# Gate projections from split operands and a new order of the middle part, in the two-layer stage of a one-core kernel

## The chip, the core and the metric

The kernel runs on one core of a Trainium2 chip. The metric is the device time of one execution in microseconds (us), given as the median of several runs. The engines are named as in the profile: PE (TensorE, matrix products), PEld (its weight loads), DVE (VectorE), ACT (ScalarE), POOL (GpSimd) and SP (SyncE, whose queue issues the DMAs here). An fp32 matmul leaves two records in the trace; a matmul of operands of type fp32r leaves one.

## What is computed

A model of two blocks on 256 tokens of width 1024. The first block (a mixer and a mixture of 32 experts) isn't touched by the change. The second block is two layers of this form:

```
def second_block(x, ...):
    for l in range(2):
        h = rms_norm_2(x, attn_norm_g[l])
        proj = h @ w_in[l]
        c_q, c_kv, k_rope, gq, gk, gv, pool_in, gate_logits = split_columns(proj, IN_SIZES)
        o_mla = mla_branch(c_q, c_kv, k_rope, ...)      # 8 heads of 96 (64 + 32 rotated)
        o_gqa = gqa_branch(gq, gk, gv, ...)             # 8 query heads of 64, 2 key heads
        o_pool = pool_branch(pool_in, w_pool[l], pool_scale[l])
        gates = jax.nn.sigmoid(gate_logits).reshape(b, s, 3, d)
        merged = (gates[:, :, 0] * (o_mla @ w_branch_mla[l])
                  + gates[:, :, 1] * (o_gqa @ w_branch_gqa[l])
                  + gates[:, :, 2] * (o_pool @ w_branch_pool[l]))
        x = x + merged @ w_out[l]
        hf = rms_norm_2(x, ffn_norm_g[l])
        u = depthwise_conv(hf @ ffn_w_up[l], ffn_conv_w[l], ffn_conv_b[l])
        x = x + (jax.nn.silu(u_gate) * u_val) @ ffn_w_down[l]
```

In both attention branches each query head and each key head is divided by its own root mean square, scaled by a gain and rotated; the softmax runs over all 256 tokens. All inputs and outputs are fp32.

## The kernel before

Activations lie with their channels over the partitions and the 256 tokens along the row, so a tile is 128 channels by 256 tokens. The layers start at 1237.7 us in the profiled execution and end with it. Five instruction streams are written out by hand, one for each engine, and meet by counting semaphores; no planner orders them.

**PSUM.** The list `order` (from L486) names every filling of one of the eight banks in the order in which PE makes them, and the engine (ACT or DVE) that takes it out. Banks go round; `lay(name)` on PE waits until the bank's last content is taken. `full(name)` on ACT and DVE waits for PE.

**Fills of a layer**, in PE's order: `ss1` and `cq`, `ckv` (latents), `gq0`, `gq1`, `gk`, `gv`, `po0`, `po1`; sums of squares `sslat`, `ssg0`, `ssg1`, `ssgk`; `ga0`, `ga1`; `uq0` to `uq3` (the mla queries), `uk0` to `uk3`, `uv0`, `uv1`; `swg0`, `swg1`, `swgk` (partners for the rotation of gq and gk); `pl0`, `pl1`; `ga2`; `ssq0` to `ssq3`; `ga3`, `ga4`; `ssk0` to `ssk3`; `ga5`, `ga6`; `swq0` to `swq3`, `swk0` to `swk3`; `ga7`; then the attention loop. A step i of that loop makes the scores of head i, the transposes of head i-2, in steps 0 to 3 also the gate `ga(8+i)`, and every second step the outputs of two heads. After it come the branch products `br`, the output projection `wo`, and the feed-forward part with `up0` to `up21` and `dn0` to `dn3`.

**Gates.** `gates(n)` makes one of twelve pairs of tiles of the gate logits: 2 x 8 fp32 matmuls of 128x128 weights by 256 tokens. They need only h and their weights. ACT takes them out with a tanh.

**Norms.** For queries and keys alike PE sums the squares of a head over the partitions with a matrix of ones, so that the sum stands in every partition; DVE takes mean and reciprocal over [96, 8 x 256] (mla) or [128, 6 x 256] (gq and gk), ACT takes the root, DVE multiplies the head by it. In the loop DVE takes the maximum of a head's scores (`tensor_reduce`), negates and scales it (`nmax`), ACT takes the exponential with an immediate scale and the negated maximum as bias, and sums it.

**Split operands.** The up and down projections are already made from split operands: ACT rounds a unit of weights to fp32r (`w_hi`, two buffers), DVE subtracts (`w_lo`), and PE adds hi*hi, hi*lo and lo*hi. ACT may write a buffer when PE has done with its last content.

**Weights in the ring.** `Stream` lays the pieces of weights one after another into a ring of LRING = 16384 columns and wraps; SP loads a piece when those under it are used (`used`), strictly in order. Pieces of a layer without such a predecessor in the same layer are loaded ahead (`early`): `w_lat`, `w_gq`, `w_gkv`, `w_pool`, `w_uq`. A `gate` piece holds three gates (3 MB), an `up` piece two fills (2 MB).

## Time and profile before

| | |
|---|---|
| median of 3 runs | 2229.58 us (2224.77 to 2230.18) |
| the profiled execution | 2224.29 us, its span 2222.5 us |
| mean granted clock of PE in it | 0.989 |
| PE busy | 2122.2 us, 95% |
| DVE busy | 812.7 us, 37% |
| ACT busy | 540.9 us, 24% |
| the layers | from 1237.7 us to the end |

The chain of work that ended last is PE for 69% of the span. A row of the order of time gives start, duration, engine, line, operation, what it writes and reads, shape, count, and in brackets the idle time before it with what ended it. The last records' ends of PE are modelled, so the spacing of starts tells more than the duration of one.

### The profile page before, as it was taken

The numbers are of one execution on the slowest core, as the hardware profiler recorded it, in microseconds if no ns is written. First come the engines' busy times: TensorE is split into PE (matmuls) and PEld (weight loads), VectorE is DVE, ScalarE is ACT, GpSimd is POOL, SyncE is SP. The second block draws the span as 40 slices with busy tenths as digits, with TensorE's granted clock in tenths as the row PEclk, the third lists the DMA queues.
The fourth block names the chain that finished last, engine by engine and source line by source line (L and its number), as shares of the span: only waits on it lengthen the run. The fifth ranks groups of instructions, "written<-read, shape, count | busy, mean of one in ns | idle before, by whom it ended". The sixth has DMA issues, their size and how long they took to land.

```text
span 2222.5 us, 29751 instructions
## 1 busy us (share of the span) xinstructions
PE 2122.2 (95%) x11486; PEld 1333.1 (60%) x11487; DVE 812.7 (37%) x1468; ACT 540.9 (24%) x905; POOL 25.3 (1%) x45
## 2 busy tenths in 40 slices
PE   6998999999999999999999999999999999999999
PEld 4763333333333333333333787778999887688999
DVE  3521221122222112221121348434885258425874
ACT  1421111111111111111111122312663132403653
POOL 0000000000000000000000020000000020000000
PEclk8998999999999999999999999999999999999999
DMA  9686997099999999999899334316551633325551
GB/s 347 254 353 255 410 419 303 1 381 418 418 417 417 417 419 418 418 418 418 334 417 411 106 114 152 114 40 199 178 194 53 199 112 118 114 97 169 190 176 53
DMA packets 210004, 580.05 MB, mean 261 GB/s; under 512 B 23264, under 2 KB 124896, under 8 KB 173952
## 3 DMA queue, kind: packets, MB, share of 16 engines
q1 hardware_dynamic: 209920, 578.83, 67.9%
q8 instruction: 65, 1.06, 0.2%
q14 instruction: 19, 0.16, 0.0%
HBM read 577.48 MB, written 1.31 MB: 260 GB/s over the span
## 4 chain that ended last, share of the span: by engine, by line
PE 69%; DMA 10%; SPq 8%; DVE 8%; ACT 3%; issue 2%; ACTq 0%; DVEq 0%
PE bank L756 16%; PE bank L1017 13%; DMA ring<-in_w_gu 9%; PE bank L1068 8%; SPq L630 4%; SPq L632 4%; PE bank L1340 3%; PE bank L1342 3%; PE bank L1341 3%; PE bank L980 3%; PE bank L994 3%; DVE heap L2104 2%; PE bank L826 2%; DMA ring<-in_w_in 2%; PE bank L1356 1%
## 5 line engine op out<-in xcount | busy, mean ns | idle before, releaser
L1017 PE MATMUL bank<-ring,heap 128*64 128x512 f32 x2304 | 519.2, 601 | 23.9 <-DMA ring<-in_w_gu 23.8
L1017 PEld LDWEIGHTS bank<-ring,heap 128*64 128x64 f32 x2304 | 158.0, 138 | 367.2 <-issue 289.2
L756 PE MATMUL bank<-heap,ring 128*128 128x256 f32 (+1 forms) x1600 | 350.5, 380 | 5.3 <-DVE heap L2148 3.2
L756 PEld LDWEIGHTS bank<-heap,ring 128*128 128x128 f32 (+1 forms) x1600 | 301.0, 189 | 51.5 <-DVE heap L2148 4.0
L1939 DVE TENSOR_SCALAR heap<-bank 128x256 f32<-128x256 f32 x36 | 15.3, 425 | 744.9 <-PE bank L1017 744.9
L1068 PE MATMUL bank<-ring,heap 128*64 128x512 f32 x1152 | 255.1, 595 | 0.0
L1340 PE MATMUL bank<-h_hi,w_hi 128*128 128x256 f32 x640 | 181.7, 284 | 3.4 <-DVE w_lo L2161 3.4
L1342 PE MATMUL bank<-h_hi,w_lo 128*128 128x256 f32 x640 | 181.1, 283 | 0.0
L1341 PE MATMUL bank<-h_lo,w_hi 128*128 128x256 f32 x640 | 181.1, 283 | 0.0
L2161 DVE TENSOR_TENSOR w_lo<-ring,w_hi 128x2048 fp32r<-128x2048 f32 (+1 forms) x64 | 142.4, 2226 | 97.7 <-ACT w_hi L1635 97.7
L1068 PEld LDWEIGHTS bank<-ring,heap 128*64 128x64 f32 x1152 | 79.3, 137 | 150.2 <-issue 144.2
L1491 ACT ACT_TABLE_LOAD x32 | 41.1, 1283 | 485.5 <-DVE heap L1939 485.0
L1635 ACT ACTIVATE w_hi<-ring 128x2048 fp32r<-128x2048 f32 (+1 forms) x64 | 119.1, 1861 | 145.2 <-PE bank L1342 85.5
L1340 PEld LDWEIGHTS bank<-h_hi,w_hi 128*128 128x128 f32 x640 | 122.8, 192 | 3.9 <-DVE w_lo L2161 3.8
L1341 PEld LDWEIGHTS bank<-h_lo,w_hi 128*128 128x128 f32 x640 | 122.8, 192 | 0.1
L1342 PEld LDWEIGHTS bank<-h_hi,w_lo 128*128 128x128 f32 x640 | 122.8, 192 | 0.0
L1356 PE MATMUL bank<-f_hi,w_hi 128*128 128x256 f32 x352 | 100.0, 284 | 1.0 <-DVE w_lo L2161 1.0
L1357 PE MATMUL bank<-f_lo,w_hi 128*128 128x256 f32 x352 | 99.6, 283 | 0.0
L1358 PE MATMUL bank<-f_hi,w_lo 128*128 128x256 f32 x352 | 99.6, 283 | 0.0
L1505 ACT ACTIVATE heap<-bank 128x512 f32<-128x512 f32 x36 | 21.5, 598 | 231.5 <-PE bank L1068 231.5
L980 PE MATMUL bank<-heap 128*64 128x512 f32 x296 | 73.4, 617 | 3.5 <-DVE heap L1899 3.5
L994 PEld LDWEIGHTS bank<-heap 64*128 64x128 f32 x592 | 54.1, 186 | 35.8 <-issue 29.2
(299 smaller groups left out, 2321.9 us busy)
## 6 DMA issues: line engine op xcount, KB each, us to landing
ring<-in_w_gu SPq DMA_DIRECT2D x256, 1024.0 KB, 18.8
ring<-in_w_down SPq DMA_DIRECT2D x128, 1024.0 KB, 19.8
ring<-in_ffn_w_up SPq DMA_DIRECT2D x44, 1024.0 KB, 7.7
ring<-in_w_ada SPq DMA_DIRECT2D x24, 1024.0 KB, 10.6
ring<-in_w_in SPq DMA_DIRECT2D x24, 1024.0 KB, 7.9
ring<-in_ffn_w_down SPq DMA_DIRECT2D x16, 1024.0 KB, 6.0
ring<-in_w_in SPq DMA_DIRECT2D x7, 2048.0 KB, 12.2
ring<-in_w_out SPq DMA_DIRECT2D x6, 2048.0 KB, 12.8
```

Source lines behind the costliest of these rows:

```text
L756: last = mm(outp, w(k), x(k), start=k == 0, stop=k == nk - 1)
L980: last = mm(psum[2][both[f], :], pick[:, t, FEW * r:FEW * (r + 1)], htok[:, t, 512 * f:512 * (f + 1)], start=t == 0, stop=t == TT - 1)
L994: last = mm(acc_of(f, c), y_sb[both[f], P * c:P * (c + 1)], sgT[both[f], :], start=False, stop=True, skip_group_check=True)
L1017: last = mm(psum[g][both[f], :], xgT[:, k % 4, k // 4, :], wt[:, g, :, f, :], start=False, stop=k == DT - 1, skip_group_check=True)
L1068: last = mm(psum[2][both[f], :], hidT[:, o:o + FEW], wt[:, 512 * f:512 * (f + 1)], start=k == 0, stop=k == DT - 1)
L1340: mm(b[:, g, :], wh, h_hi[:, k, :], start=k == 0, stop=False)
L1341: mm(b[:, g, :], wh, h_lo[:, k, :], start=False, stop=False)
L1342: last = mm(b[:, g, :], wl, h_hi[:, k, :], start=False, stop=k == DT - 1)
L1356: mm(b[:, a, :], wh, f_hi[:, k, :], start=k == 0 and a == 0, stop=False, skip_group_check=True)
L1357: mm(b[:, a, :], wh, f_lo[:, k, :], start=False, stop=False, skip_group_check=True)
L1635: f(hi, src, ACT.Copy).then_inc(S["whi"].sem, 1)
L2161: v.tensor_tensor(lo, src, hi.bitcast(F32), ALU.subtract).then_inc(S["wlo"].sem, 1)
```

## The change

1. **Gates from split operands.** `gates(n)` now makes three products of fp32r operands: 48 matmuls. Before it, ACT rounds the piece `ga{n}` to `w_hi` (`lead_gate`) and DVE makes `w_lo` (`rest_gate`). h itself is split once per layer. `lead_gate(n+2)` follows on ACT when gate n is taken out.
2. **Query norms.** Queries are multiplied by their gain only. Their sums of squares are made with tokens over the partitions (`by_query`: the squares as weights, one or two columns of ones), [128, 16] for all heads; reciprocal and root are taken of that, and the factor (with 1/sqrt of the head size) becomes the scale of the exponential and of `nmax`. Keys keep their norm.
3. **New order** of the fills between `uv1` and the attention loop, and of DVE's and ACT's work to match. DVE's steps between the `rest_gate` calls, which the diff below leaves out, are: before `rest_gate(1)` the mean and reciprocal of `sslat`; before `rest_gate(2)` cq and ckv scaled, mean and reciprocal of `ssgq` and `ssgk`, gq times its gain, gk scaled; before `rest_gate(4)` the means of `ssk0` to `ssk3`; before the long reciprocal the products of `swg0`, `swg1`, `swgk` and of `swq0` to `swq3` with the sine table; before `rest_gate(6)` mk scaled, the pool outputs, gq and gk times cosine and the sums; before `rest_gate(7)` the same for mq; after it `swk0` to `swk3` and the rotation of mk. Each `rest_gate` waits for its `lead_gate`.
4. **Smaller ring**: LRING = 10240; a gate, branch, output or half query/pool piece is 1 MB. `early` is now `w_lat`, `w_gq0`, `w_gq1`. The exponentials, their transposes and h lie in buffers of other steps. The down projection's four banks are 3, 4, 5, 6.

```diff
-LRING = 16384
+LRING = 10240
+NG = 12
@@ order of the fills
-                 ("gv", "act"), ("po0", "act"), ("po1", "act"), ("sslat", "dve"), ("ssg0", "dve"), ("ssg1", "dve"),
+                 ("gv", "act"), ("po0", "act"), ("po1", "act"), ("sslat", "dve"), ("ssgq", "dve"),
                  ("ssgk", "dve"), ("ga0", "act"), ("ga1", "act")]
         order += [(f"uq{i}", "act") for i in range(4)] + [(f"uk{i}", "act") for i in range(4)]
-        order += [("uv0", "act"), ("uv1", "act")] + [("swg0", "dve"), ("swg1", "dve"), ("swgk", "dve")]
-        order += [("pl0", "dve"), ("pl1", "dve"), ("ga2", "act")] + [(f"ssq{i}", "dve") for i in range(4)] + [("ga3", "act"), ("ga4", "act")]
-        order += [(f"ssk{i}", "dve") for i in range(4)] + [("ga5", "act"), ("ga6", "act")]
-        order += [(f"swq{i}", "dve") for i in range(4)] + [(f"swk{i}", "dve") for i in range(4)] + [("ga7", "act")]
+        order += [("uv0", "act"), ("uv1", "act"), ("ssq", "dve"), ("ga2", "act")] + [(f"ssk{i}", "dve") for i in range(4)]
+        order += [("swg0", "dve"), ("swg1", "dve"), ("swgk", "dve")] + [(f"swq{i}", "dve") for i in range(4)]
+        order += [("pl0", "dve"), ("pl1", "dve"), ("ga3", "act"), ("ga4", "act"), ("ga5", "act")]
+        order += [(f"swk{i}", "dve") for i in range(4)] + [("ga6", "act"), ("ga7", "act")]
...
+        def gate_unit(n):
+            hi, lo = (x[:, n % 2, :].rearrange("p (a b) -> p a b", a=DT) for x in (w_hi, w_lo))
+            return piece(lay_stream, f"ga{n}", DT), hi, lo
@@ used(name): when a piece may be overwritten
+            if name.startswith("ga"):
+                return S["wlo"], int(name[2:]) + 1
@@ PE
                 def gates(n):
-                    if n % 3 == 0:
-                        arrived(f"gate{n // 3}")
-                    w = piece(lay_stream, f"gate{n // 3}", 8, 3)
+                    done("wlo", n + 1)
+                    _, hi, lo = gate_unit(n)
                     b = halves(lay(f"ga{n}"))
                     for a in range(2):
-                        last = product(b[:, a, :], lambda k: w[:, k, n % 3, P * a:P * (a + 1)], h, DT)
+                        for k in range(DT):
+                            wh, wl = hi[:, k, P * a:P * (a + 1)], lo[:, k, P * a:P * (a + 1)]
+                            mm(b[:, a, :], wh, h_hi[:, k, :], start=k == 0, stop=False)
+                            mm(b[:, a, :], wh, h_lo[:, k, :], start=False, stop=False)
+                            last = mm(b[:, a, :], wl, h_hi[:, k, :], start=False, stop=k == DT - 1)
...
+                def by_query(name, slots, rows, sums):
+                    b = lay(name)
+                    n = 2 * NH // (TT * slots)
+                    for t in range(TT):
+                        for i in range(slots):
+                            o = NH * t + n * i
+                            last = mm(b[:, o:o + n], rows(i)[:, P * t:P * (t + 1)], sums, start=True, stop=True)
+                    last.then_inc(lay_full.sem, 1)
@@ ACT
+                def lead_gate(n):
+                    src, hi, _ = gate_unit(n)
+                    act.wait_ge(*lay_in.here(f"ga{n}", l))
+                    f(hi, src, ACT.Copy).then_inc(S["whi"].sem, 1)
                 def gates(n):
                     o = 8 * (n % 3) + 2 * (n // 3)
                     out_of(f"ga{n}", L["gates"][:, o:o + 2, :], func=ACT.Tanh, scale=0.5)
+                    if n + 2 < NG:
+                        lead_gate(n + 2)
...
                 for i in range(4):
-                    out_of(f"uq{i}", L["mq"][0:MQ, 2 * i:2 * i + 2, :], lambda b: two(b)[0:MQ])
+                    b = two(full(f"uq{i}"))[0:MQ]
+                    f(L["mq"][0:MQ, 2 * i:2 * i + 2, :], b, ACT.Identity, scale=v2("q_head", 0)[0:MQ])
+                    f(L["sq"][0:MQ, 2 * i:2 * i + 2, :], b, ACT.Square).then_inc(lay_drained["act"].sem, 1)
...
-                        f(pr[:, 0, :], b[:, 0, :], ACT.Exp, scale=scale, bias=st[:, 2:3], accum_out=st[:, 4:5])
+                        f(pr[:, 0, :], b[:, 0, :], ACT.Exp, scale=scale[:, 0:1], bias=st[:, 2:3], accum_out=st[:, 4:5])
@@ DVE, from the latent sums on
+                rest_gate(0)
...
+                rest_gate(1)
...
+                rest_gate(2)
+                taken(mean(rq[:, 0, :], full("ssq")[:, 0:2 * NH], MQ))
+                v.reciprocal(rq[:, 0, :], rq[:, 0, :]).then_inc(S["qvar"].sem, 1)
+                rest_gate(3)
...
+                rest_gate(4)
...
+                v.reciprocal(L["rs"][0:MQ], L["rs"][0:MQ]).then_inc(S["kvar"].sem, 1)
+                rest_gate(5)
...
+                rest_gate(6)
...
+                rest_gate(7)
...
                 for i in range(2 * NH + 1):
                     if i < 2 * NH:
                         b = full(f"s_{att[i]}")
                         c.step(v.tensor_reduce(st[:, 0:2], two(b), AX.X, ALU.max))
-                        v.tensor_scalar(st[:, 2:4], st[:, 0:2], -scale, None, ALU.mult).then_inc(S["nmax"].sem, 1)
+                        v.scalar_tensor_tensor(out=st[:, 2:4], in0=st[:, 0:2], scalar=-1.0, in1=scale, op0=ALU.mult,
+                                               op1=ALU.mult).then_inc(S["nmax"].sem, 1)
+                    if i < 4:
+                        rest_gate(8 + i)
                     if i >= 1:
                         out_act(f"s_{att[i - 1]}")
```

## Rows read from the trace of the kernel before

**Rows 1.** The page, part 1: busy us, share of the span, instructions
```profile
PE 2122.2 (95%) x11486; PEld 1333.1 (60%) x11487; DVE 812.7 (37%) x1468; ACT 540.9 (24%) x905; POOL 25.3 (1%) x45
```
**Rows 2.** Stretches: us, PE, PEld, DVE, ACT, POOL busy, PEclk, DMA, GB/s
```profile
1290.00:1424.05 134.05, 128.99 (x580) 105.21 (x578) 81.39 (x61) 35.51 (x52) 12.08 (x18) 0.99 0.31 103
1781.00:1915.00 134.00, 128.94 (x579) 105.26 (x577) 81.40 (x61) 35.50 (x52) 12.08 (x18) 0.99 0.31 103
```
**Rows 3.** Order of time, PE in both layers: start, us, what, [idle before]
```profile
1311.77 7.15 PE L756 MATMUL bank<-heap,ring 128*96 128x256 f32 x32 [0.55 <-DVE heap L2028]
...
1335.49 3.62 PE L756 MATMUL bank<-heap,consts_sb 96*96 96x256 f32 x16
1338.95 13.98 PE L756 MATMUL bank<-heap,ring 128*128 128x256 f32 x64
...
1356.61 5.38 PE L756 MATMUL bank<-heap,consts_sb 96*96 96x256 f32 x16 [3.69 <-ACT heap L1598]
...
1380.09 3.69 PE L558 MATMUL bank<-heap,consts_sb 96*96 96x256 f32 x16 [0.82 <-DVE heap L2028]
...
1847.66 5.38 PE L756 MATMUL bank<-heap,consts_sb 96*96 96x256 f32 x16 [3.69 <-ACT heap L1598]
```
**Rows 4.** A stretch after the wait of 3.69 us, as in rows 2
```profile
1358.00:1360.00 2.00, 2.00 (x6) 1.28 (x6) 1.20 (x2) 1.98 (x3) 0.00 (x0) 0.50 0.02 4
```
**Rows 5.** Order of time, PE at the first split products of the up projection
```profile
1546.40 0.28 PE L1341 MATMUL bank<-h_lo,w_hi 128*128 128x256 f32 x1
...
1557.68 0.28 PE L1342 MATMUL bank<-h_hi,w_lo 128*128 128x256 f32 x1
```
**Rows 6.** Order of time, ACT and DVE: splitting a unit of weights
```profile
1555.39 1.90 ACT L1635 ACTIVATE w_hi<-ring 128x2048 fp32r<-128x2048 f32 x1
...
1561.95 2.29 DVE L2161 TENSOR_TENSOR w_lo<-ring,w_hi 128x2048 fp32r<-128x2048 f32 x1
```
**Rows 7.** Order of time, PE: products with 32 columns, two records each
```profile
167.65 0.38 PE L964 MATMUL bank<-heap,consts_sb 128*128 128x32 f32 x2 [0.21 <-issue]
167.86 0.39 PE L965 MATMUL bank<-heap,consts_sb 128*128 128x32 f32 x2
```
**Rows 8.** Order of time, DVE: key norm's reciprocal; maximum and negation of scores
```profile
1362.75 12.95 DVE L2104 RECIPROCAL heap<-heap 96x2048 f32<-96x2048 f32 x1
...
1399.95 0.69 DVE L2127 TENSOR_REDUCE heap<-bank 128x2 f32<-128x512 f32 x1 [5.17 <-PE bank L1267]
1400.67 0.17 DVE L2128 TENSOR_SCALAR heap<-heap 128x2 f32<-128x2 f32 x1
1400.75 0.16 DVE L2132 RECIPROCAL heap<-heap 128x2 f32<-128x2 f32 x1
```
**Rows 9.** Lines 1660 and 1614 (durations ns min/median/max); ACT between two heads
```profile
L1660 ACT ACTIVATE heap<-bank,vec x80: 541/554/563, 1557.2 to 2157.0; 128x256 f32<-128x256 f32 x80
L1614 ACT ACTIVATE heap<-bank,heap x32: 476/476/477, 1394.9 to 1943.6; 128x256 f32<-128x256 f32 x32
1433.59 0.48 ACT L1614 ACTIVATE heap<-bank,heap 128x256 f32<-128x256 f32 x1 [1.29 <-DVE heap L2128]
```
**Rows 10.** PE's waits of 3.17 and 2.04 us, and stretches after waits (PEclk)
```profile
215.04 0.79 PE L1009 MATMUL bank<-bias_hi,bias_sel 64*128 64x512 f32 x1 [3.17 <-issue]
219.00:221.00 2.00, 2.00 (x8) 0.51 (x6) 0.00 (x0) 0.00 (x0) 0.00 (x0) 0.50 0.39 156
1231.56 1.10 PE L1109 MATMUL bank<-heap,consts_sb 128*128 128x256 f32 x4 [2.04 <-ACT heap L1526]
1231.50:1235.00 3.50, 2.36 (x9) 1.49 (x10) 3.50 (x13) 2.53 (x4) 0.00 (x0) 1.00 1.04 380
```
**Rows 11.** Line 695, four of the five w_gkv DMAs of each layer
```profile
DMA to landing us min/median/max: 4.4/9.2/13.7
```
**Rows 12.** The page, part 6: issues, KB each, median us to landing
```profile
ring<-in_ffn_w_up SPq DMA_DIRECT2D x44, 1024.0 KB, 7.7
ring<-in_w_in SPq DMA_DIRECT2D x24, 1024.0 KB, 7.9
```

## What I expect of the change, and why

> **What bounds the kernel now.** I read the busy shares of the page, then the stretches by stage, then the order of time on PE, DVE and ACT inside a layer. TensorE is busy 95% of the span [rows 1]. The change touches the layers alone, and there I look at the part from the squared sums to the last gate projection, 1293.4 to 1424.05: PE is busy for 129.0 of 134.1 us, DVE for 81.4, ACT for 35.5, and the second layer repeats it to a tenth [rows 2]. PE stands still three times in it, 0.55, 3.69 and 0.82 us, for DVE or ACT [rows 3]. After the 3.69 us its granted clock is 0.50, the 1.2 GHz level [rows 4], and 16 records take 5.38 us where 16 like them took 3.62 [rows 3]: 1.76 more. So PE sets the time, and DVE's chain of norms already touches the path.
>
> **The change part by part**, for one layer; the two layers double it.
>
> *Gates.* Two gate projections, 64 records, take 13.98 us [rows 3], 6.99 each. Three products of split operands are 48 records. The up projection has this form: from its second matmul at 1546.40 to its 96th at 1557.68 lie 94 starts [rows 5], 0.12 us each, so 5.76 per gate. Twelve gates: 12 x 1.23 = 14.8 us off PE. Each gate adds 1.90 us on ACT (the rounded half) and 2.29 on DVE (the rest) [rows 6], 22.8 and 27.5 together. The split of h adds as much once, while PE works on the pool projection and DVE has nothing else: no cost.
>
> *Query norms.* The gq sums go from 4 matmuls to 8 with two columns, the mq sums from 8 to 16 with one column. Nearest row: weights of 128x128 with 32 columns, two records in 0.21 us, 0.107 each [rows 7]. gq: 8 x 0.2185 = 1.75 becomes 16 x 0.107 = 1.71. mq: 5.38 becomes 32 x 0.107 = 3.42. Ends: 7.0 if a record cost as much as one of 256 columns (0.2185), 1.7 if it cost half of the nearest row; I take 3.42, the row with weights of the same width. Saved: 2.0. On DVE one of the two 12.95 us reciprocals [rows 8], its four means and its scaling go, and most of the one for gq/gk; tiny ones replace them. The factor now enters the exponential as a second operand per partition: activations out of PSUM with two such operands take 554 ns, with one 476 [rows 9]. That is 0.16 per head on ACT, which idles 1.29 ahead of a pair [rows 9]: no cost; without that cover 16 heads x 0.16 = 2.5. The Trainium skill (ScalarE: Activation LUTs, on what an ACTIVATE costs) gives about 93 ns for each such operand. By it the uncovered price would be 3.0; the rows have 78 ns.
>
> *Old waits.* 0.55 + 3.69 + 0.82 = 5.1 us go: the latent norm no longer stands behind the gq/gk reciprocal, the mk squares and the mk norm no longer behind those of mq.
>
> What goes: 14.8 + 2.0 + 5.1 = 21.9 us per layer, 43.8 in all.
>
> *New waits.* Every gate now waits for DVE's rest, so DVE's order counts. I lay the new order on layer 0's clock. PE: sums until 1297.3 as before, gates 0 and 1 until 1308.8 (their rests are ready at 1284 and 1301), uq 7.0, uk 3.6, uv 1.8, ssq 3.4, gate 2 5.8, ssk 3.5: 1333.9. From there DVE carries the chain: mean 0.7, rest of gate 4 2.2, three swg 1.9, four swq 2.4, reciprocal of mk 12.9 [rows 8], rest of gate 5 2.3: 1356.3. PE meanwhile does swg, swq and pool (7.8) and gates 3 and 4 (11.5), is ready for gate 5 at 1353.3 and waits 3.0. Then mk scaled 2.3, pool 1.6, rotation of gq/gk 3.6, rest of gate 6 2.3: 1366.0, PE waits 0.4. Rotation of mq 4.5, rest of gate 7 2.3: 1372.7, PE waits 1.0. swk and rotation of mk until 1379.6, when PE has just done the first scores. If the clock falls after the 3.0 wait, the lost 1.76 goes into the next two waits and leaves 0.4.
> The first four attention steps are the worst place. PE issues the scores of head i and then gate 8+i; on DVE the rest of gate 8+i stands behind maximum and negation of these same scores, and behind it stand the normalisation of the head before and that head's transposes. From the end of the scores: 0.72 + 0.08 + 2.29 = 3.1 us [rows 6, 8]. In steps 0 and 1 PE has nothing beside it; in steps 2 and 3 the transposes cover 0.5. New waits: 3.1 + 3.1 + 2.6 + 2.6 = 11.4, where the kernel before had none.
> All new waits are 3.0 + 0.4 + 1.0 + 11.4 = 15.8, with the 0.4 left over 16.2. Gained: 21.9 - 16.2 = 5.7 us per layer; the last gate would end at 1418.4.
>
> *The clock.* What does a wait of 3.1 or 2.6 us cost beyond itself? After waits of 3.17 and 3.69 the granted clock was 0.50, after one of 2.04 it was 1.00 [rows 4, 10]. 3.1 lies beside 3.17; 2.6 lies halfway. I take 2.5 half-speed stretches per layer in these four steps, at 1.76 each: 4.4 us. Bounds: none, or all four (7.0). Left: 5.7 - 4.4 = 1.3 per layer, 2.6 in all.
> The Trainium skill (TensorE: Matmul & The Clock Gate, on HAM oscillation) warns of idle gaps between short bursts of matmuls that put the engine back to half rate each time. It speaks against this change, and the 5.38 us row agrees.
>
> *Smaller ring.* 10240 columns hold five pieces of 1 MB. w_gkv is no longer loaded ahead: it waits for ckv and is needed two tile pairs (14.0 us) later. Its 256 KB DMAs landed 4.4 to 13.7 us after issue, beside other loads [rows 11]. With five issues of about 1 us ahead of the last, 5 + 9.2 would just miss, but those landings were in a crowded queue; alone I take 5 + 5: no cost. At worst 5 + 13.7 - 14.0 = 4.7 per layer. Behind it in SP's queue stand w_po0, w_po1 and gate 0, each needed 8 us or more after issue, against a median of 7.9 for such pieces [rows 12]. The third up piece now waits for up1, done at 1546.4; its user on ACT started at 1555.39 [rows 5, 6]; median landing 7.7 [rows 12]: no cost, at worst (13.7) 4.7. Later up pieces have some 17 us, three units of 5.76, between release and use.
>
> *The rest.* The new banks of the down projection, the exponentials and their transposes in the places of rs and sq, and branch and output weights in halves keep order and work: nothing. The three-operand negation on two elements: 0 to 0.1 us a head.
>
> **The sum.** The profiled execution took 2224.3 us (span 2222.5); 2224.3 - 2.6 = 2221.7 on that footing. The median of the three runs, 2229.6, lies 5.3 above it, so I forecast 2229.6 - 2.6 = 2227.0. A difference below 0.3% (6.7 us) can't be told from none here.
>
> **The rivals.**
> (a) The waits stay but the clock doesn't fall: 11.4 gained, 2218.2. For it: the 2.04 row. Against it: the 3.17 row. Chance 0.24.
> (b) PE never waits for the rests, and all 43.8 come: 2185.8. DVE's order as written speaks against it. Chance 0.04.
> (c) The other side: in the first four attention steps each wait is followed by a half-speed stretch like the one after 3.17 us, which held from 215 to 221 [rows 10], worth 3.0. Eight waits x 3.0 = 24.0 against 11.4: 12.6 slower, 2242.2. It decides from 18.1 (11.4 + 6.7), six such waits. The one-column sums, 3.4 us of weight loads with hardly a column, could add 1.76 per layer. Against it: the two 3.69 waits inside the layers lost 1.76 each. Chance 0.12.
> (d) The smaller ring starves PE at w_gkv and at the third up piece: 2 x (4.7 + 4.7) = 18.8 against 2.6: 16.2 slower, 2245.8. Chance 0.08.
>
> **How the numbers follow.** The forecast has 0.52: 2227.0, own range 2221 to 2236 (all four stretches in both layers, -11.4 + 14.1, and 3.5 for the one-column sums give +6.2). Faster: (a) and (b), 0.28. Same: the forecast, 0.52. Slower: (c) and (d), 0.20. The range takes in (a) with the runs' spread of 5 below it, and reaches toward (c): 2214 to 2238, which leaves out (b), (d) and most of (c).
>
> **What would show it.** Gate records start 0.12 apart; 384 f32 records per layer give way to 576 split ones. PE waits for the rests some 16 us per layer: 3.1, 3.1, 2.6 and 2.6 in the first four attention steps, about 3 before gate 5; after some of them slices at 0.50. uq starts near 1308.8, the last gate ends between 1418 and 1425. The prediction is wrong if PE doesn't wait in those four steps, if the clock stays at 1.00 after 3.1 us, or if PE waits for the ring.

## The result, and the profile after

The changed kernel takes 2232.25 us at the median of 20 runs (2224.51 to 2238.12), the kernel before 2229.34 (2223.9 to 2231.06, 20 runs). The ratio is 1.002, interval 1.001 to 1.0029: some 4.5 us slower (2.2 to 6.5). The forecast was 2.6 us faster. The time lies in the range given, but the direction was wrong. By the bound of 0.3% it is no difference; by the interval it is a small loss.

The profiled execution took 2233.18 us against 2224.29 for the one of before. Of these 8.9 us, 1.1 lie ahead of the layers (the first projection of layer 0 starts at 1238.78 instead of 1237.67), 3.8 in the first layer up to its branch products and 3.9 from there to the same point of the second layer. The rest lies behind that. The profiled execution of before was quick beside its 20 runs. So the layers are the place, and both show nearly the same loss.

The page of the kernel after, part 1, to be read beside [rows 1]:
```profile
PE 2110.7 (95%) x11918; PEld 1345.7 (60%) x11919; DVE 822.4 (37%) x1486; ACT 586.7 (26%) x939; POOL 31.1 (1%) x45
```
PE has 432 records more: 2 x 192 for the gates and 2 x 24 for the query sums. It is nevertheless busy for 11.5 us less. What was taken off it came back as waits and as time at half speed (time at half speed counts as busy).

PE's waits after, from the middle of the expert part to the end (waiting line, releaser, us in total, times, longest):
```profile
PE bank L1167 <- DVE w_lo L2101: 30.5, 12, 3.3
...
PE bank L1180 <- DMA ring<-in_w_in: 0.2, 1, 0.2
```
L1167 is the first product of a gate, L2101 DVE's rest: 30.5 us in twelve waits. Before, this wait did not exist. PE itself waits for a transfer only once in the layers, for 0.2 us; before it was 0.5. The ring of 10240 columns shows in one other place. In layer 0 ACT waits 0.38 us for the third up piece, and PE, which waits for that piece's rest at the first up product, waits 2.19 us where it waited 1.72 before:
```profile
1560.77 1.91 ACT L1669 ACTIVATE w_hi<-ring 128x2048 fp32r<-128x2048 f32 x1 [0.38 <-DMA ring<-in_ffn_w_up]
...
1565.06 0.39 PE L1362 MATMUL bank<-h_hi,w_hi 128*128 128x256 f32 x1 [2.19 <-DVE w_lo L2220]
```

Order of time on PE in layer 0 after (start, us, line, [idle before]):
```profile
1309.92 7.07 PE L770 MATMUL bank<-heap,ring 128*96 128x256 f32 x32
...
1322.34 4.51 PE L1218 MATMUL bank<-consts_sb,heap 96*128 96x1 f32 x32
...
1334.73 3.62 PE L770 MATMUL bank<-heap,consts_sb 96*96 96x256 f32 x16
...
1360.52 0.39 PE L1167 MATMUL bank<-h_hi,w_hi 128*128 128x256 f32 x1 [2.89 <-DVE w_lo L2101]
...
1376.86 0.39 PE L1167 MATMUL bank<-h_hi,w_hi 128*128 128x256 f32 x1 [0.70 <-DVE w_lo L2101]
...
1382.00 0.28 PE L1167 MATMUL bank<-h_hi,w_hi 128*128 128x256 f32 x1
1382.36 0.28 PE L1167 MATMUL bank<-h_hi,w_hi 128*128 128x256 f32 x1
...
1387.21 0.58 PE L1167 MATMUL bank<-h_hi,w_hi 128*128 128x256 f32 x1 [3.28 <-DVE w_lo L2101]
...
1388.02 0.41 PE L1167 MATMUL bank<-h_hi,w_hi 128*128 128x256 f32 x1
1388.66 0.41 PE L1167 MATMUL bank<-h_hi,w_hi 128*128 128x256 f32 x1
...
1400.06 0.58 PE L1167 MATMUL bank<-h_hi,w_hi 128*128 128x256 f32 x1 [3.18 <-DVE w_lo L2101]
...
1411.75 0.38 PE L1167 MATMUL bank<-h_hi,w_hi 128*128 128x256 f32 x1 [2.60 <-DVE w_lo L2101]
...
1422.01 0.38 PE L1167 MATMUL bank<-h_hi,w_hi 128*128 128x256 f32 x1 [2.60 <-DVE w_lo L2101]
...
1427.94 1.13 PE L1290 MATMUL bank<-heap 64*128 64x256 f32 x4
```
The upper rows are uq, the one-column sums and, behind gate 2, the first of the key sums. The waits stand where they were forecast, at gates 5 and 7 and at gates 8 to 11. L1167 is every third record of a gate: in gate 7 two such starts lie 0.36 us apart, 0.12 per record, and in gate 8, behind the wait of 3.28, they lie 0.64 apart.

Stretches of the same layer after (from:to, length, PE, PEld, DVE, ACT and POOL busy, granted clock, DMA share, GB/s):
```profile
1320.00:1334.00 14.00, 14.00 (x81) 12.66 (x80) 2.57 (x3) 6.92 (x9) 0.00 (x0) 0.76 0.49 151
1356.00:1366.00 10.00, 7.11 (x59) 6.91 (x58) 10.00 (x9) 5.60 (x4) 0.00 (x0) 1.00 0.44 130
1384.00:1396.00 12.00, 8.79 (x49) 8.66 (x50) 3.05 (x3) 2.54 (x6) 0.00 (x0) 0.72 0.28 87
1398.00:1410.00 12.00, 9.10 (x56) 8.34 (x56) 4.13 (x6) 3.80 (x8) 0.00 (x0) 0.86 0.29 89
1410.00:1428.00 18.00, 13.65 (x105) 12.76 (x105) 6.29 (x8) 3.82 (x11) 0.00 (x0) 1.00 0.34 118
```
A mean clock of 0.72 over 12 us means (1 - 0.72) x 12 / 0.5 = 6.7 us at 1.2 GHz. In this way: 6.7 us at the one-column sums and gate 2 (PE busy throughout!), none behind the 2.89 us at gate 5, 6.7 behind the 3.28 us at gate 8, 3.4 behind the 3.18 us at gate 9, none behind the two of 2.60. The second layer has the same three stretches. In the trace's record of the clock the lengths are 6.83, 6.83 and 3.41 us, so 17.1 us per layer; before it was one of 3.41 per layer [rows 4].

What the stretches cost is read from starts. The first and the last record of a gate start 5.74 us apart in gates 10 and 11, at full clock, 8.33 in gate 8 and 7.18 in gate 9: 2.6 and 1.4 us lost, 4.0 together. From the start of the one-column sums to the end of gate 2 it is 12.39 us (1322.34 to 1334.73), where the same work at full clock takes 9.33 (e1's second layer, below): 3.1 lost. So the clock costs 7.1 us of the layer, less than half of 17.1, since the starts of a gate's records go from 0.12 to 0.21 apart and not to 0.24.

Line 1648, the exponential, after (durations in ns, min/median/max), to be read beside [rows 9]:
```profile
L1648 ACT ACTIVATE heap<-bank,heap x32: 557/564/566, 1385.2 to 1952.2; 128x256 f32<-128x256 f32 x32
```
564 ns where it was 476.

### The profile page after: what moved, and what is told of

Read it like the earlier page. It is cut to its first block, busy times and chain, and to the rows that moved or that the text cites. A ratio compares the mean times of both kernels' runs of the same rounds, so it can differ in the third digit from the quotient of the medians.

```text
span 2231.3 us, 30713 instructions
## 1 busy us (share of the span) xinstructions
PE 2110.7 (95%) x11918; PEld 1345.7 (60%) x11919; DVE 822.4 (37%) x1486; ACT 586.7 (26%) x939; POOL 31.1 (1%) x45
## 4 chain that ended last, share of the span: by engine, by line
PE 72%; DMA 11%; DVE 7%; SPq 6%; ACT 2%; issue 2%; ACTq 0%; DVEq 0%
PE bank L1031 15%; PE bank L770 12%; DMA ring<-in_w_gu 9%; PE bank L1082 9%; SPq L643 4%; PE bank L1362 3%; PE bank L1363 3%; PE bank L1364 3%; PE bank L994 3%; PE bank L1008 3%; PE bank L840 2%; PE bank L1167 2%; PE bank L1168 2%; PE bank L1169 2%; DMA ring<-in_w_in 2%
## 5 line engine op out<-in xcount | busy, mean ns | idle before, releaser
L1973 DVE TENSOR_SCALAR heap<-bank 128x256 f32<-128x256 f32 x36 | 15.3, 424 | 745.1 <-PE bank L1031 745.1
L770 PE MATMUL bank<-heap,ring 128*128 128x256 f32 (+2 forms) x832 | 183.2, 380 | 4.2 <-DVE heap L2207 3.1
L1362 PE MATMUL bank<-h_hi,w_hi 128*128 128x256 f32 x640 | 181.7, 284 | 3.9 <-DVE w_lo L2220 3.9
L1363 PE MATMUL bank<-h_lo,w_hi 128*128 128x256 f32 x640 | 181.1, 283 | 0.0
L1364 PE MATMUL bank<-h_hi,w_lo 128*128 128x256 f32 x640 | 181.1, 283 | 0.0
L770 PEld LDWEIGHTS bank<-heap,ring 128*128 128x128 f32 (+2 forms) x832 | 152.9, 185 | 32.1 <-DVE heap L2207 4.0
L1167 PE MATMUL bank<-h_hi,w_hi 128*128 128x256 f32 x384 | 117.1, 305 | 30.8 <-DVE w_lo L2101 30.5
L1362 PEld LDWEIGHTS bank<-h_hi,w_hi 128*128 128x128 f32 x640 | 122.8, 192 | 4.3 <-DVE w_lo L2220 4.3
L1168 PE MATMUL bank<-h_lo,w_hi 128*128 128x256 f32 x384 | 114.2, 297 | 0.0
L1169 PE MATMUL bank<-h_hi,w_lo 128*128 128x256 f32 x384 | 113.8, 296 | 0.0
L1167 PEld LDWEIGHTS bank<-h_hi,w_hi 128*128 128x128 f32 x384 | 79.7, 207 | 35.1 <-DVE w_lo L2101 35.0
```

Source lines behind the costliest of these rows:

```text
L770: last = mm(outp, w(k), x(k), start=k == 0, stop=k == nk - 1)
L1167: mm(b[:, a, :], wh, h_hi[:, k, :], start=k == 0, stop=False)
L1168: mm(b[:, a, :], wh, h_lo[:, k, :], start=False, stop=False)
L1169: last = mm(b[:, a, :], wl, h_hi[:, k, :], start=False, stop=k == DT - 1)
L1362: mm(b[:, g, :], wh, h_hi[:, k, :], start=k == 0, stop=False)
L1363: mm(b[:, g, :], wh, h_lo[:, k, :], start=False, stop=False)
```

## The experiments

The theory that I went into them with (A): the four waits of the attention steps, the clock behind them, and the clock at the one-column sums carry the loss. The rival (B) differs by run and stands in the expectations. For comparing single profiles I use two stretches that leave out what lies ahead of the layers: from the first projection of layer 0 to its first branch product (first stretch), and from there to the same point of layer 1 (second). They are start times of rows of the order of time, subtracted:

| kernel | first stretch, us | second, us |
|---|---|---|
| before | 220.37 | 491.05 |
| after | 224.17 | 494.97 |
| rests ahead (e1) | 207.81 | 475.59 |
| filled waits (e2) | 220.21 | 491.93 |
| wide sums (e3) | 223.64 | 491.73 |
| mixed sums (e4) | 222.04 | 491.53 |
| constant scale (e5) | 221.70 | 494.87 |
| ahead and mixed (e6) | 204.86 | 477.17 |
| filled and mixed (e7) | 217.22 | 488.77 |
| ahead and wide (e8) | 204.87 | 477.37 |
| first two half filled (e9) | 222.78 | 493.35 |

**e1: the rests of gates 8 to 11 ahead of the steps that need them.**
```diff
                 turned("k", "rs")
+                rest_gate(8)
...
-                    if i < 4:
-                        rest_gate(8 + i)
                     if i >= 1:
                         out_act(f"s_{att[i - 1]}")
...
+                    if i < 3:
+                        rest_gate(9 + i)
```


> Edit to the changed kernel: on DVE the rest of gate 8 is made right after the four swk products, and the rests of gates 9, 10 and 11 at the end of attention steps 0, 1 and 2, ahead of the next scores' maximum. Nothing else moves. Against the changed kernel (2232.3 us): Theory A (waits and the clock that falls with them): the waits of 3.28, 3.18, 2.60 and 2.60 us go in both layers (23.3 us) and with them the half-speed stretches of 6.8 and 3.4 us at the first two (worth 5.1 per layer, 10.2 in all): about 2199 us, slices of PE after the first scores at a granted clock of 1.00. Theory B (the clock is not tied to these waits; gates run slow there for another reason, say two engines reading the same memory): only the waits go, about 2209, and slices at 0.50 stay in the gates 8 and 9.


Measured: 2200.87 us (2196.88 to 2204.28), ratio 0.9889 [0.9872, 0.9905]. A holds. PE's waits for a rest, and the attention steps of layer 0:
```profile
PE bank L1167 <- DVE w_lo L2101: 6.5, 3, 2.9
...
1382.00:1411.00 29.00, 29.00 (x220) 26.88 (x218) 15.70 (x19) 13.36 (x25) 0.00 (x0) 1.00 0.42 146
```
PE is busy for all of the 29 us, at full clock; three waits of twelve are left, all ahead of the attention steps. In its second layer the clock stays up at the sums, so their price at full clock can be read there:
```profile
1800.39 3.63 PE L1218 MATMUL bank<-consts_sb,heap 96*128 96x1 f32 x32
```
Gate 2 starts at 1803.89, and what follows it at 1809.72, 9.33 us behind the first start. The same work with DVE's instructions in another order is 0.0111 x 2229 = 25 us faster than the kernel before, and (1.002 - 0.9889) x 2229 = 29 us faster than the changed one.

**e2: PE works in the waits.** Products whose result the gate's own first product overwrites fill the four waits; DVE's order stays.
```diff
-                def gates(n):
+                def gates(n, extra=0):
-                    done("wlo", n + 1)
-                    _, hi, lo = gate_unit(n)
                     b = halves(lay(f"ga{n}"))
+                    for m in range(extra):
+                        mm(b[:, 0, :], h_hi[:, m % DT, 0:P], h_hi[:, m % DT, :], start=True, stop=True)
+                    done("wlo", n + 1)
+                    _, hi, lo = gate_unit(n)
...
-                        gates(i + 8)
+                        gates(i + 8, (24, 24, 20, 20)[i])
```


> Edit to the changed kernel: ahead of its wait for the rest of gates 8 to 11, PE makes 24, 24, 20 and 20 matmuls of fp32r operands from h_hi into the bank that the gate then overwrites (2.9, 2.9, 2.4, 2.4 us at 0.12 each). The waits for DVE stay as long as they are, but PE is busy in them. Theory A (the clock falls because PE stood idle): the start of each gate stays where it is, the granted clock stays at 1.00, gates 8 and 9 take 5.8 us each: 5.1 us less per layer, about 2222 us. Theory B (clock not tied to the idle time): no change, 2232. If the filling overruns a wait, each gate starts up to 0.3 us later: up to 2 us more.


Measured: 2226.75 (2221.7 to 2231.75), ratio 0.9999 [0.9988, 1.001]: 0.0021 below the ratio of the change, 4.7 us. By the trace the two stretches are 4.0 and 3.0 shorter than after. The attention steps:
```profile
1386.00:1430.00 44.00, 43.26 (x324) 39.84 (x324) 17.06 (x21) 13.84 (x26) 0.00 (x0) 1.00 0.30 97
```
Clock 1.00 in 44 us. So the clock behind the waits is worth 4.0 us per layer, apart from the waits, since the filling lets no gate start before its rest is made. That is what the starts in gates 8 and 9 gave for the kernel after (2.6 + 1.4). My expectation of 5.1 took half of the 10.2 us at half speed. In the second layer it is 3.0, as there the clock now fell behind gate 5's wait for 3.4 us.

**e4: the one-column sums among gate 2's products**, two after each triple of gate 2 instead of 32 in a block.
```diff
-                by_query("ssq", NH, lambda i: L["sq"][0:MQ, i, :], const("ones", 1)[0:MQ, :])
-                gates(2)
+                sums = lay("ssq")
+                done("wlo", 3)
+                _, hi, lo = gate_unit(2)
+                b = halves(lay("ga2"))
+                for a in range(2):
+                    for k in range(DT):
+                        for o in range(2 * (DT * a + k), min(2 * (DT * a + k) + 2, 2 * NH)):
+                            t, i = divmod(o, NH)
+                            ins = mm(sums[:, o:o + 1], L["sq"][0:MQ, i, P * t:P * (t + 1)], const("ones", 1)[0:MQ, :],
+                                     start=True, stop=True)
...
```


> Edit to the changed kernel: the 16 one-column matmuls of the mla query sums are issued two at a time among the first 24 matmuls of gate 2, and no longer in one block ahead of it. Same instructions. Now block and gate take 4.4 + 8.0 = 12.4 us with 6.8 us at 0.50. Theory A (a stretch with hardly a column lets the clock fall, as idle time does): the clock stays at 1.00, both take 9.2 us, 3.2 less per layer, about 2226 us. Theory B (one-column matmuls are slow in themselves, 0.137 us a record, and gate 2 is slow for another reason): 12.4 us stay, 2232. In both the squares of mk start some 4 us later, which may let PE wait up to 1 us ahead of ssk.


Measured: 2228.88 (2224.74 to 2234.93), ratio 1.001 [0.9998, 1.0021]: 0.001 below the change's ratio, with intervals that overlap. The time alone would decide nothing; the trace does:
```profile
1322.00:1334.00 12.00, 12.00 (x89) 10.83 (x90) 2.57 (x3) 7.08 (x9) 0.00 (x0) 1.00 0.56 176
1356.00:1366.00 10.00, 7.17 (x37) 7.18 (x38) 9.96 (x11) 5.59 (x4) 0.00 (x0) 0.66 0.35 105
```
At the sums the clock stays at 1.00. But now it falls behind the 2.89 us wait at gate 5, for 6.8 us, where the changed kernel had 1.00 behind the same wait. There it costs less: gate 5 loses 2.65 us, but PE afterwards no longer waits the 0.70 us for gate 7. The stretches are 2.1 and 3.4 shorter than after.

**e3: the same block with 32 columns of ones.**
```diff
-                by_query("ssq", NH, lambda i: L["sq"][0:MQ, i, :], const("ones", 1)[0:MQ, :])
+                b = lay("ssq").rearrange("p (a b) -> p a b", b=32)
+                for t in range(TT):
+                    for i in range(NH):
+                        last = mm(b[:, NH * t + i, :], L["sq"][0:MQ, i, P * t:P * (t + 1)], const("ones", 32)[0:MQ, :],
+                                  start=True, stop=True)
+                last.then_inc(lay_full.sem, 1)
```


> Edit to the changed kernel: the 16 matmuls of the mla query sums have 32 columns of ones instead of one. Theory A1 (what counts for the clock is how many columns stream): 32 columns at 0.107 us a record are a quarter of what a record of 128 columns has; if that is enough the block takes 3.4 us and gate 2 5.8 at 1.00; if it is not, 12.4 us in all as now. Theory A2 (what counts is whether matmuls are in flight at all): then one column would have done, and the fall has another cause; no change to expect, 12.4 us.


The block, what follows gate 2, and the stretch around them:
```profile
1322.44 3.66 PE L1248 MATMUL bank<-consts_sb,heap 96*128 96x32 f32 x32
...
1331.76 3.62 PE L770 MATMUL bank<-heap,consts_sb 96*96 96x256 f32 x16
...
1320.00:1334.00 14.00, 14.00 (x99) 12.05 (x98) 3.57 (x5) 9.05 (x11) 0.00 (x0) 1.00 0.49 151
```
32 times the columns, and the block is shorter (3.66 instead of 4.51 us), as the clock stays up; block and gate 2 take 9.32 us instead of 12.39. The one execution took 2229.52 us, which decides nothing; the second stretch is 3.2 shorter than after, the first only 0.5, since there the clock fell behind gates 5, 10 and 11 as well.

**e5: a constant for the query norm factor** in the exponentials and the negated maxima (the factor 1/rms is left out of the result).
```diff
-                        scale = two(L["rq"][:, 0 if att[i][0] == "m" else 1, :])[:, :, int(att[i][1])]
+                        scale = (MQ if att[i][0] == "m" else HD) ** -0.5
...
-                        f(pr[:, 0, :], b[:, 0, :], ACT.Exp, scale=scale[:, 0:1], bias=st[:, 2:3], accum_out=st[:, 4:5])
+                        f(pr[:, 0, :], b[:, 0, :], ACT.Exp, scale=scale, bias=st[:, 2:3], accum_out=st[:, 4:5])
```


> The changed kernel with a constant in place of the query norm factor in the exponentials and in the negated maxima: the factor 1/rms of the queries is left out of the result, and nothing is put in its place. Each exponential then has one operand per partition instead of two. Theory A (the second operand, 0.078 us each by the rows of the trace before, is on the path of the attention steps that only ACT sets, behind the last gate): pairs of heads in these steps stand 4.73 apart again instead of 4.90, and from the last gate's end to the first branch product it takes 34.0 us instead of 35.15: 1.2 less per layer, 2.3 in all. Theory B (it is ACT's slack, and the longer spacing comes from the new bank order): 4.90 stays.


The exponential in it, and transposes of two successive pairs, first in it, then in the kernel after:
```profile
L1648 ACT ACTIVATE heap<-bank,heap x32: 465/473/474, 1382.7 to 1948.9; 128x256 f32<-128x256 f32 x32
...
1440.62 0.66 PE L1298 MATMUL bank<-consts_sb,heap 128*128 128x128 f32 x4 [0.48 <-DVE heap L2192]
...
1445.34 0.66 PE L1298 MATMUL bank<-consts_sb,heap 128*128 128x128 f32 x4 [0.48 <-DVE heap L2192]
```
```profile
1443.32 0.66 PE L1298 MATMUL bank<-consts_sb,heap 128*128 128x128 f32 x4 [0.48 <-DVE heap L2193]
...
1448.22 0.66 PE L1298 MATMUL bank<-consts_sb,heap 128*128 128x128 f32 x4 [0.48 <-DVE heap L2193]
```
4.72 apart without the second operand, 4.90 with it. From the scores behind the last gate to the first branch product it is 34.0 us (1425.60 to 1459.55) instead of 35.0; before it was 34.0. A holds: the operand lengthens these steps. The size is 1.0 us per layer, not the 1.2 that I had expected, and the time of a single execution (2229.7) says nothing on 2 us.

**e6 and e8: both repairs together**, e1 with e4, and e1 with e3; no edit beyond theirs.


> The changed kernel with both repairs: DVE's rests of gates 8 to 11 are made ahead of the attention steps, and the one-column sums stand two at a time among gate 2's matmuls. Theory A (the four waits and the one-column sums each cost what their own runs showed, and the two add up): the first repair alone gave 2200.9, the second alone 3.4 less than the changed kernel; together 2200.9 - 3.4 = 2197.5, and no slice at 0.50 between the squared sums and the last gate projection. Theory B (the clock only falls elsewhere instead, as it did after the 2.9 us wait ahead of gate 5 when the sums alone were mixed): the second repair gives back up to 3.4 per layer on PE at that wait: 2201 to 2204. Against the kernel before (2229.3): A a ratio of 0.9857, B 0.987 to 0.989.

> The rests of gates 8 to 11 made ahead, and the mq sums with 32 columns of ones instead of one (the same 32 records, 3.66 us in the look at it, no slice at 0.50 there). Theory A (a block of records with 32 columns keeps the clock up, and nothing else is left for it to fall at but gate 5's wait): 2200.9 - 3.4 + 2 x 0.2 = 2197.9, as good as mixing the sums. Theory B (the clock then falls after gate 5's 2.9 us wait in both layers, as it did in the look at the wide sums): 2201 to 2204.


Measured: e6 2195.56 us (2194.84 to 2201.59), ratio 0.9866 [0.9849, 0.9883]; e8 2196.27 (2195.65 to 2201.11), ratio 0.9867 [0.9851, 0.9883]. The kernel before took 2226.41 in this round. On these times e6 lies at the edge between A (0.9857) and B (0.987). The trace of e6 is B's:
```profile
1320.00:1334.00 14.00, 14.00 (x100) 12.48 (x99) 4.63 (x6) 9.05 (x9) 0.00 (x0) 1.00 0.49 151
1354.00:1364.00 10.00, 7.82 (x51) 7.71 (x52) 9.97 (x11) 5.86 (x5) 0.00 (x0) 0.83 0.34 105
1378.00:1407.00 29.00, 29.00 (x220) 26.91 (x219) 16.46 (x19) 13.37 (x25) 0.00 (x0) 1.00 0.42 146
```
No fall at the sums and none in the attention steps, but 3.4 us at half speed behind gate 5's wait; e8 is the same. In the first stretch both are 2.9 shorter than e1. In the second they are 1.6 and 1.8 longer. e1's own second layer had no fall at its sums, so nothing was to be gained there; and in both e6 and e8 the clock also fell for 3.4 us in the first layer's feed-forward part, behind a wait of 2.16 and 2.24 us at the first up product, where e1 waited 2.11 and stayed at 1.00. Both beat the kernel before by 1.3%, and they are the fastest that I ran; which of them is better can't be told.

**e7: e2 and e4 together**: the gates still wait for their rests, and the clock's losses at the sums and in the attention steps are taken away.


> The changed kernel with its DVE order as it is: PE still has to wait for all four rests, but works in these waits on 24, 24, 20 and 20 products whose result is thrown away, and the one-column sums are mixed into gate 2. So only the clock's part of the cost is taken away, at both places. Theory A (the time lost beyond the waits is the clock's: 5.1 us per layer after the waits and 3.4 at the sums): 2232.3 - 5.5 (filled waits alone) - 3.4 (mixed sums alone) = 2223.4, and slices of 1.00 throughout both stretches. Theory B (the filling hides it, but the clock falls at the 2.9 us wait ahead of gate 5 in both layers): 2226 to 2227, and a stretch at 0.50 behind gate 5's wait.


Measured: 2223.03 us (2221.69 to 2227.78), ratio 0.9986 [0.9978, 0.9995]. Against the change's 1.002 that is 0.0034, 7.6 us; by the stretches 7.0 and 6.2 per layer. At its sums the clock stays at 1.00 (1320 to 1334). Around gate 5 and in the attention steps:
```profile
1354.00:1364.00 10.00, 7.02 (x46) 6.85 (x45) 9.96 (x11) 5.60 (x4) 0.00 (x0) 0.83 0.36 107
1378.00:1421.00 43.00, 42.27 (x320) 39.23 (x319) 16.89 (x20) 13.37 (x26) 0.00 (x0) 1.00 0.30 99
```
B was right that the clock falls at gate 5 instead, A nearly right on the gain. This is the run that answers for the sign: with the gates as late as DVE makes them, but the clock up in those two places, the change would be faster than the kernel before by 0.05 to 0.22%.

**e9: does the length of a single wait decide?** As e2, with 12, 12, 0 and 0 products (one execution, 2230.6 us).


> The changed kernel, where PE works in the waits ahead of gates 8 and 9 on 12 products whose result is thrown away (some 1.5 us), so that of each of these waits about half is left; the waits ahead of gates 10 and 11 stay at 2.6 us with nothing in them. Theory A (it is the length of the single wait: those of 3.3 and 3.2 us let the clock fall, those of 2.6 do not): no slice at 0.50 from 1385 to 1428, and the last gate ends as early as with all four waits filled, some 5 us before the changed kernel's counted from the layer's start. Theory B (waits close behind one another let it fall, so the pair of 2.6 us does it once the first two no longer have): a slice at 0.50 between gates 10 and 11, and 1.7 to 3.4 us of the 5 are not gained.


Gates 10 and 11 of its layer 0, and the stretches around gates 8 and 9, 10, and 11:
```profile
1404.68 0.55 PE L1169 MATMUL bank<-h_hi,w_hi 128*128 128x256 f32 x1 [2.69 <-DVE w_lo L2103]
...
1417.61 0.55 PE L1169 MATMUL bank<-h_hi,w_hi 128*128 128x256 f32 x1 [2.68 <-DVE w_lo L2103]
...
1378.00:1403.00 25.00, 20.80 (x151) 18.59 (x150) 10.92 (x13) 9.59 (x15) 0.00 (x0) 1.00 0.26 86
1403.00:1415.00 12.00, 10.24 (x56) 9.51 (x56) 2.93 (x4) 1.97 (x6) 0.00 (x0) 0.72 0.26 88
1415.00:1424.00 9.00, 6.39 (x41) 6.42 (x42) 3.20 (x5) 1.69 (x5) 0.00 (x0) 0.81 0.35 118
```
A falls, B holds. Behind the half filled waits the clock stays at 1.00, but now it falls behind waits of 2.7 us, which had left it at 1.00 in the kernel after (2.60): 6.7 us behind gate 10, 3.4 behind gate 11, together as much as before the filling. The starts in gates 10 and 11 give 2.6 and 1.4 us lost, 4.0 as before. The first stretch is 1.4 shorter than after, but that comes from its sums, where the clock fell for 3.4 instead of 6.8 us (10.82 us for sums and gate 2 instead of 12.39). So the half filling gained nothing: all of the 4.0 us was lost elsewhere, more than the 1.7 to 3.4 that B had. A wait of 2.6 us brought a fall in e3's first layer (gates 10 and 11) and in e5's second (gate 10) too, with the longer waits in their places. Whether it does so isn't set by its length.

## Why the prediction was wrong, point by point

**The gates' products** (14.8 us per layer): nearly right, some 13. 0.12 us per record holds within a gate. But a gate also has a slower first record, and the fp32 gate was priced by its busy time, not by starts. From a gate's start to the next work's start it is 7.00 us before and 5.93 after at full clock (1422.01 to 1427.94), 1.1 less and not 1.23:
```profile
1417.05 7.07 PE L756 MATMUL bank<-heap,ring 128*128 128x256 f32 x32
1424.05 1.13 PE L1267 MATMUL bank<-heap 64*128 64x256 f32 x4
```
uq was to start near 1308.8; it starts at 1309.92 in an execution whose layer begins 1.1 later, so at 1308.8.

**The new waits** (15.8 us, and 0.4 left over): right within 1 us. Forecast were 3.0, 0.4 and 1.0 at gates 5, 6 and 7, and 3.1, 3.1, 2.6, 2.6 at gates 8 to 11. Measured: 2.89, none, 0.70, and 3.28, 3.18, 2.60, 2.60, together 15.3. They come from DVE's order as read from the code: maximum, negation, rest, and only then the head before.
```profile
1396.92 0.69 DVE L2183 TENSOR_REDUCE heap<-bank 128x2 f32<-128x512 f32 x1 [9.76 <-PE bank L1290]
1397.64 0.16 DVE L2184 SCALAR_TENSOR_TENSOR heap<-heap 128x2 f32<-128x2 f32 x1
1397.72 2.28 DVE L2101 TENSOR_TENSOR w_lo<-ring,w_hi 128x2048 fp32r<-128x2048 f32 x1
1399.92 0.16 DVE L2191 RECIPROCAL heap<-heap 128x2 f32<-128x2 f32 x1
```
These are rows of step 1 of layer 0 after: DVE has stood idle for 9.76 us, and then makes PE wait for a 2.28 us instruction that it could have done in that time. e1 does just that.

**The smaller ring and its transfers** (0; rival (d)): right but for 0.5 us in one layer, at the third up piece that (d) names.

**The clock** is the step that failed, and it failed at the one-column sums: their effect on it was put at nothing in the sum, and left to rival (c) with 1.76 us. The runs show 3.1 us per layer, the largest error in the sum.
- The one-column sums were costed at 3.42 us by their records. That price was right at full clock (3.63 us of busy time, 3.50 from start to start, in e1's second layer). But the clock fell in the block and stayed down through most of gate 2: 6.8 us, 3.1 lost. PE was busy without a break there, for 4.5 us of the block, but on weight loads with a single column each. Such a block brought a fall in 8 of the 10 layers that had it (after, e1, e2, e5, e9), the mixed or widened one in none of 10 (e3, e4, e6, e7, e8). Two different edits that take the block away or widen it keep the clock up there, so this cause is shown.
- In the attention steps the forecast was 2.5 stretches of 1.76 us, 4.4 per layer. Measured is 4.0, so the size came out right, but by luck, since neither the number nor the price of the stretches was right: there were two, one of 6.83 us that cost 2.6 and one of 3.41 that cost 1.4. In [rows 10] there was such a long one behind 3.17 us, and I had kept it for rival (c).

I took from [rows 4, 10] that the length of a wait decides, with a point somewhere between 2.04 and 3.17. The same place as the row of 2.04 us contradicts this. In the kernel after the wait there is 2.03 us, and the clock behind it is 0.50:
```profile
1232.66 4.51 PE L1123 MATMUL bank<-heap,consts_sb 128*128 128x256 f32 x12 [2.03 <-ACT heap L1548]
...
1233.00:1236.00 3.00, 3.00 (x8) 2.08 (x8) 3.00 (x11) 2.33 (x4) 0.00 (x0) 0.50 0.00 0
```
So it is in four of the ten profiles of the new order (after, e1, e2, e4); it costs nothing there, 6.12 us from this row to the first projection against 6.11 before. The Trainium skill (TensorE: Matmul & The Clock Gate, on HAM oscillation) warns of idle gaps between bursts of matmuls. The trace agrees for gates 8 and 9 and not for gates 10 and 11, and in e9 it is the other way round, with waits of nearly the same length at gates 10 and 11. The same page (Part 1: The HAM clock gate) says of a kernel's start that the number of slow matmuls varies between runs of one kernel. That fits what e1 shows inside a kernel: its two layers have the same instructions, and one falls at the sums, the other at gate 5.

**The exponential's second operand** was put at zero because ACT idles 1.29 us ahead of a pair [rows 9]. That idle time is itself a wait for DVE, in a round of ACT, DVE and PE that paces the steps behind the last gate. The round is my reading of the rows; that the steps lengthen with the operand and shorten without it, e5 shows. The text had the price without cover, 2.5 us per layer; measured is 1.0. The row [rows 9] gave 0.078 us per operand, the runs give 0.088 to 0.091 (564 against 476 and 473 ns). The 93 ns that the Trainium skill gives for a pointer operand (ScalarE: Activation LUTs, What ACT_TABLE_LOAD costs) would have been nearer than my row.

**The sum again**, per layer. The forecast gain was 1.3. Off it go 3.1 for the clock at the sums, 1.8 for the gates' products, 1.0 for the exponentials and 0.2 for the sums' own price; to it come 0.9, as the waits were 15.3 and not 16.2, and 0.4, as the clock in the attention steps was 4.0 and not 4.4. That makes a loss of 3.5; the table has 3.8 and 3.9. The 3.1 can be seen by itself: on the clock of [rows 2] (1.1 taken off) gate 5 was to start at 1356.3 and starts at 1359.4. Without the 3.1 the layer would still have been some 0.7 slower than before: the gates and the exponentials have their part in the sign. Both layers give 7.7 us in the profile. The medians show 4.5 (2.2 to 6.5): the two profiled executions differ by more than the kernels do, and which part of the 7.7 is luck of one execution stays open. The stretches at half speed are the likely place, since they vary between layers with equal instructions.

**The rivals.** (a), the clock doesn't fall, had 0.24. It had the waits right and the clock wrong; e7 shows that it would have meant a gain. (c) was half right: the longer stretches and the one-column sums were its own, but in two of four waits per layer instead of in all. A forecast of the likeliest case that took the sums' term from (c) would have had the sign right (2.6 - 3.5), short of the size. (b) had 0.04; e1 shows that with four of DVE's rests moved the kernel gets 25 of its 43.8 us. (d) showed in 0.5 us.

## What to carry to other kernels

When work is moved from a busy engine to a helper, the place in the helper's instruction stream matters as much as its price: a rest that takes 2.3 us, on an engine that had just idled 9.8, cost PE a wait in each of four steps because it stood behind the wrong instruction. A block of matmuls with one column each should be costed with the clock it leaves behind; mixing it with other products, or widening it to 32 columns, cost PE no time here (9.3 us with gate 2 either way) and kept the clock up there. Part of the gain went again where the clock then fell behind the next wait, so that a repair is judged by the whole layer. An engine's idle time covers an addition only if the wait in it isn't part of the round that the engine itself is in.

## What the runs showed of the hardware that I had not expected

- TensorE's clock fell to its lower level (0.50 granted) while the engine was busy throughout, in blocks of 32 records with one column (96 x 128 weights). 32 records with 32 columns took 3.66 us and left it up.
- Waits of equal length gave different clocks: 2.89 us at gate 5 was followed by 1.00 in the kernel after and by 0.66 over 10 us in e4, and 2.03 us ahead of the layers by 0.50 in the kernel after and by 1.00 in e5. In the 20 layers run with the new order, gate 5's wait was followed by a fall in 11 of the 12 without a fall at the sums before it, and in 1 of the 8 with one (e2's second layer). Why an earlier fall spares a later one, no run here shows.
- Within the layers a stretch at half speed was 3.4 or 6.8 us long, and which of the two it was varied for the same place (3.4 us at the sums in e5, 6.8 in the kernel after). A stretch of 3.4 us cost 1.4 us of gate products, whose starts went from 0.12 to 0.21 us apart.
- An exponential with two operands per partition took 564 ns, with one 473 to 476, at 128 x 256 out of PSUM.
